# Retention stage: gate projections moved between scores, value products and sums; squares added on VectorE; the input norm's root carried by the rotary tables, decays and gates

## The reference

```python
h = rms_norm_2(x, mix_norm[i])                 # x * rsqrt(mean(x*x)) * gain
q, k, v, g = split(h @ w_in)                   # 4 heads: q, k 256 wide, v, g 512 wide
q = rotary(q, pos); k = rotary(k, pos) / 16
scores = (q . k) * decay                       # chunk-causal, decay by head
o = scores @ v
o = rms_norm_2(o, out_gain) * silu(g)          # norm over the 512 columns of a head
x = x + o @ w_o
```

## Time and profile before

| | |
|---|---|
| median of 3 runs | 3081.96 us (3081.77 to 3082.68) |
| profiled execution | 3082.99 us |
| its span, first to last instruction | 3081.2 us |
| mean granted TensorE clock | 0.982 |
| TensorE busy | 2969.8 us, 96% |
| VectorE busy | 1184.6 us, 38% |
| ScalarE busy | 569.9 us, 18% |
| GpSimd busy | 1822.2 us, 59% |

### The profile page before, as it was taken

One profiled execution on the slowest core, in us unless ns is written; L12 is line 12 of the kernel. 1 busy time (PEld: TensorE's weight loads), 2 busy tenths in 40 slices (PEclk: granted clock), 3 DMA queues, 4 the chain that ended last, 5 costly groups with the idle time before them and its releaser, 6 DMA issues.

```text
span 3081.2 us, 36748 instructions
## 1 busy us (share of the span) xinstructions
PE 2969.8 (96%) x13812; PEld 2373.5 (77%) x13812; DVE 1184.6 (38%) x1400; ACT 569.9 (18%) x787; POOL 1822.2 (59%) x1822
## 2 busy tenths in 40 slices
PE   6999998999998999999999989999999999999999
PEld 4677776888875677888878868878888777788887
DVE  3467224332435564432431321254233355543141
ACT  2442212100012443100011101120001344310000
POOL 4346444777782234777775645657777634477775
PEclk8899999999998999999999999999999999999999
DMA  3112211223231011223232212212222211122322
GB/s 116 55 55 69 82 62 48 96 84 111 86 105 35 26 41 41 96 84 103 94 122 82 73 64 82 82 69 91 93 98 91 76 60 54 55 96 87 102 96 84
DMA packets 37230, 242.16 MB, mean 79 GB/s; under 512 B 4128, under 2 KB 4256, under 8 KB 15136
## 3 DMA queue, kind: packets, MB, share of 16 engines
q1 hardware_dynamic: 36288, 237.19, 22.7%
q10 hardware_dynamic: 864, 3.89, 0.4%
HBM read 238.97 MB, written 2.10 MB: 78 GB/s over the span
## 4 chain that ended last, share of the span: by engine, by line
PE 90%; DVE 4%; ACT 2%; POOL 1%; issue 1%; DMA 1%; DVEq 1%; ACTq 0%; POOLq 0%; SPq 0%
PE ps L394 62%; PE ps L416 12%; PE ps L1291 1%; PE ps L1260 1%; PE ps L1086 1%; PE ps L1223 1%; PE ps L1103 1%; PE ps L1113 1%; POOL w_lo L659 1%; PE ps L676 1%; PE ps L1277 1%; PE ps L1304 1%; PE ps L753 1%; PE ps L1209 1%; PE ps L1074 0%
## 5 line engine op out<-in xcount | busy, mean ns | idle before, releaser
L655 POOL CAST w_hi<-raw 128x512 fp32r<-128x512 f32 (+1 forms) x909 | 580.1, 679 | 1221.5 <-PE ps L394 849.8
L659 POOL TENSOR_TENSOR w_lo<-raw,w_hi 128x512 fp32r<-128x512 f32 (+1 forms) x909 | 1242.2, 1396 | 20.2
L394 PE MATMUL ps<-h_hi,w_hi 128*128 128x512 f32 x1904 | 756.3, 397 | 18.2 <-DVE h_lo L1745 9.7
L394 PE MATMUL ps<-h_lo,w_hi 128*128 128x512 f32 x1904 | 745.5, 392 | 0.0
L394 PE MATMUL ps<-h_hi,w_lo 128*128 128x512 f32 x1904 | 745.0, 391 | 0.0
L394 PEld LDWEIGHTS ps<-h_hi,w_hi 128*128 128x128 f32 x1904 | 360.8, 189 | 99.1 <-DVE h_lo L1745 10.5
L394 PEld LDWEIGHTS ps<-h_lo,w_hi 128*128 128x128 f32 x1904 | 360.7, 189 | 76.6 <-issue 3.4
L394 PEld LDWEIGHTS ps<-h_hi,w_lo 128*128 128x128 f32 x1904 | 360.2, 189 | 76.1
L394 PE MATMUL ps<-a_hi,w_hi 128*128 128x512 f32 x816 | 320.8, 393 | 6.2 <-DVE x L1937 2.9
L394 PE MATMUL ps<-a_lo,w_hi 128*128 128x512 f32 x816 | 319.4, 391 | 0.0
L394 PE MATMUL ps<-a_hi,w_lo 128*128 128x512 f32 x816 | 319.4, 391 | 0.0
(11 more groups left out here) (274 smaller groups left out, 3632.8 us busy)
## 6 DMA issues: line engine op xcount, KB each, us to landing
raw<-weights SPq DMA_DIRECT2D x169, 1024.0 KB, 4.9
raw<-weights SPq DMA_DIRECT2D x64, 704.0 KB, 4.1
raw<-weights SPq DMA_DIRECT2D x8, 640.0 KB, 3.9
raw<-weights SPq DMA_DIRECT2D x8, 512.0 KB, 3.6
x<-x_in SPq DMA_DIRECT2D x1, 2048.0 KB, 8.9
x_out<-x SPq DMA_DIRECT2D x1, 2048.0 KB, 6.3
scr<-phase_ret ACTq DMA_DIRECT2D x1, 1536.0 KB, 9.0
scr<-phase_ssd ACTq DMA_DIRECT2D x1, 640.0 KB, 4.2
```

Of the source, the lines that this page charges most:

```text
L394: mm = pe.matmul(out_ap, a, b, start=(i == 0 and not begun), stop=(i == n - 1 and ended))
L655: ins = pool.tensor_copy(w_hi[:, slot, piece], raw[:, slot, piece])
L659: ins = pool.tensor_tensor(w_lo[:, slot, piece], raw[:, slot, piece], w_hi[:, slot, piece].bitcast(F32), ALU.subtract)
```

## The change

It does five things, all within the retention stage.

1. `ret` joins `late_rstd`. TensorE takes the squares' sum after the first q projection. The root goes into the tables: VectorE multiplies `cos` and `sin` by it once; the root by token, turned onto partitions by four one-column matmuls (`r_tok`), multiplies the decays; each gate bank is multiplied by it before Silu (`g_scaled`).
2. The gate projections are cut into four banks of 24 matmuls and moved: one between scores and value products, one behind the value products, then the sum of squares, then two.
3. Scores use banks 0 to 3, and so do the four value products, which stay in PSUM until VectorE has normed them. ScalarE's copy goes.
4. The four squares are added on VectorE; TensorE sums once instead of four times.
5. The waits for `x` being updated are moved behind the k projection. The loops over two heads are written out. ScalarE loads its function tables ahead by hand.

```diff
@@ late_rstd @@
-            return name.startswith("ffn") or name in ("sb", "mla")
+            return name.startswith("ffn") or name in ("sb", "mla", "ret")
@@ TensorE, ret @@
-                pe.wait_ge(s_res, 8 * (res_before["ret"] + half) + 2)
+                    def proj_g(r, half):
+                        if half == 0:
+                            chunk_split(c + 4 + r)
+                        mm = features(pe, ps[:, 4 + 2 * r + half, :], slot[4 + r], 256, half * P, P)
+                        mm.then_inc(s_used if half else s_rgp, 1)
...
-                    pe.wait_ge(s_rg, 2 * hd + 1)
+                    if hd:
+                        pe.wait_ge(s_roo, 4 * hd)
                     features2(pe, (0, 1), slot[0], h_ready("ret")).then_inc(s_used, 1)
+                    if hd == 0:
+                        norm("ret")
                     chunk_split(c + 1)
...
+                    if j == 0:
+                        pe.wait_ge(s_res, 8 * (res_before["ret"] + half) + 2)
+                    if hd == 0:
+                        pe.wait_ge(s_rstd, norm_of["ret"] + 1)
+                        for tb in range(TB):
+                            mm = pe.matmul(ps[:, 7, tb:tb + 1], norm_rstd[:, tb * P:(tb + 1) * P], ident[:, 0:1],
+                                           start=True, stop=True)
+                        mm.then_inc(s_rtok, 1)
+                    else:
+                        pe.wait_ge(s_rgs, 4 * hd)
+                        pe.wait_ge(s_rr, hd)
...
-                    for r in range(2):
-                        chunk_split(c + 4 + r)
-                        pe.wait_ge(s_rq, 2 * hd + r + 1)
-                        features(pe, ps[:, 2 * r, :], slot[4 + r], 256, 0, P)
-                        features(pe, ps[:, 2 * r + 1, :], slot[4 + r], 256, P, P).then_inc(s_used, 1)
...
+                    pe.wait_ge(s_rv, 2 * hd + 1)
+                    proj_g(0, 0)
+                    pe.wait_ge(s_rv, 2 * hd + 2)
+                    pe.wait_ge(s_rp, 4 * hd + 4)
                     for v in range(4):
...
-                        if v:
-                            mean(v - 1)
-                    mean(3)
+                    proj_g(0, 1)
+                    pe.wait_ge(s_rgs, 4 * hd + 1)
+                    pe.wait_ge(s_radd, hd + 1)
+                    pe.matmul(ps[:, 4, :], ones, r_sq[:, 0, :], start=True, stop=True).then_inc(s_rsum, 1)
+                    proj_g(1, 0)
+                    proj_g(1, 1)
...
+                pe.wait_ge(s_rr, 2 * half + 2)
+                pe.wait_ge(s_rgs, 8 * half + 6)
@@ ScalarE, ret @@
+                    act.preload_act_table_set(LN_EXP)
                     for v in range(4):
                         act.wait_ge(s_ro, 4 * hd + v + 1)
-                        act.wait_ge(s_rsum, 4 * hd + v + 1)
-                        act.activation(r_sq, ps[:, 6 + v % 2, :], ACT.Square)
-                        act.activation(r_oo[v], ps[:, 6 + v % 2, :], ACT.Copy).then_inc(s_rsq, 1)
+                        act.activation(r_sq[:, v, :], ps[:, v, :], ACT.Square).then_inc(s_rsq, 1)
+                    act.wait_ge(s_rsum, hd + 1)
+                    rstd(r_rstd, ps[:, 4, :], 1.0 / T).then_inc(s_rr, 1)
+                    act.preload_act_table_set("silu_and_others")
+                    for v in range(4):
+                        act.wait_ge(s_rgs, 4 * hd + v + 1)
+                        act.activation(r_g[:, v, :], r_g[:, v, :], ACT.Silu).then_inc(s_rg, 1)
@@ VectorE, ret @@
+                    def g_scaled(v):
+                        if v % 2:
+                            wait_used(c + 4 + v // 2)
+                        else:
+                            dve.wait_ge(s_rgp, 2 * hd + v // 2 + 1)
+                        dve.tensor_tensor(r_g[:, v, :], ps[:, 4 + v, :], norm_rstd, ALU.mult).then_inc(s_rgs, 1)
+
+                    def out_tile(v):
+                        dve.drain()
+                        dve.wait_ge(s_rg, 4 * hd + v + 1)
+                        dve.tensor_tensor(r_oo[v], r_oo[v], r_g[:, v, :], ALU.mult)
+                        split(a_hi[:, 4 * j + v, :], a_lo[:, 4 * j + v, :], r_oo[v]).then_inc(s_mix, 1)
+
+                    if hd == 0:
+                        dve.wait_ge(s_phase, 16 * (phase_order.index("ret") + 1))
+                        dve.wait_ge(s_rstd, norm_of["ret"] + 1)
+                        dve.tensor_tensor(cos, cos, norm_rstd, ALU.mult)
+                        dve.tensor_tensor(sin, sin, norm_rstd, ALU.mult)
+                    rotary(0, r_q)
+                    if hd == 0:
+                        dve.wait_ge(s_rtok, 1)
+                        dve.tensor_copy(r_tok, ps[:, 7, 0:TB])
+                    rotary(1, r_k)
...
+                    g_scaled(0)
+                    for v in range(1, 4):
+                        dve.wait_ge(s_rsq, 4 * hd + v + 1)
+                        ins = settled().tensor_tensor(r_sq[:, 0, :], r_sq[:, 0, :], r_sq[:, v, :], ALU.add)
+                    ins.then_inc(s_radd, 1)
+                    g_scaled(1)
+                    dve.wait_ge(s_rr, hd + 1)
                     for v in range(4):
...
+                        dve.scalar_tensor_tensor(r_oo[v], ps[:, v, :], param("ret_norm", 4 * hd + v), r_rstd,
+                                                 ALU.mult, ALU.mult).then_inc(s_roo, 1)
+                    g_scaled(2)
+                    for v in range(3):
+                        out_tile(v)
+                    g_scaled(3)
+                    out_tile(3)
```

More of the change, by code:

```diff
@@ L572, in build_program @@
         s_mT, s_mp, s_mo, s_mod = (sem("mla_scores_turned"), sem("mla_exp"), sem("mla_o"), sem("mla_o_scaled"))
-        used[0] = 0
+        used[0] = T
         r_rstd = take(T)
-        r_sq = take(T)
         r_t = take(2 * T, k=2)
+        r_tok = take(TB)
         assert used[0] <= base_norm
@@ L587, in build_program @@
         r_p = take(sum(RW))
-        s_rq = sem("ret_rotated")
-        s_rv, s_rg = sem("ret_v_copied"), sem("ret_g_silu")
+        r_sq = take(4 * T, v=4)
+        s_rtok, s_rq = sem("ret_rstd_turned"), sem("ret_rotated")
+        s_rv, s_rgp, s_rgs, s_rg = (sem("ret_v_copied"), sem("ret_g_product"), sem("ret_g_scaled"), sem("ret_g_silu"))
         s_rs, s_rp = sem("ret_scores"), sem("ret_scores_decayed")
-        s_ro, s_rsq, s_rsum, s_rr, s_rdone = (sem("ret_o"), sem("ret_square"), sem("ret_square_summed"),
-                                            sem("ret_rstd"), sem("ret_head_done"))
+        s_ro, s_rsq, s_radd, s_rsum, s_rr, s_roo = (sem("ret_o"), sem("ret_square"), sem("ret_squares_added"),
+                                                   sem("ret_mean"), sem("ret_rstd"), sem("ret_o_normed"))
         r_oo = [r_q[:, 0, :], r_q[:, 1, :], r_k[:, 0, :], r_k[:, 1, :]]
@@ L1178, in head @@
                     slot = [(c0 + r) % 2 for r in range(6)]
+                    def proj_g(r, half):
[3 more added lines that the diff above has]
+                        mm.then_inc(s_used if half else s_rgp, 1)
                     chunk_split(c)
-                    pe.wait_ge(s_rg, 2 * hd + 1)
+                    if hd:
+                        pe.wait_ge(s_roo, 4 * hd)
                     features2(pe, (0, 1), slot[0], h_ready("ret")).then_inc(s_used, 1)
+                    if hd == 0:
+                        norm("ret")
                     chunk_split(c + 1)
[L1184 to L1190, removed]
+                    for k in range(2):
+                        mm = features(pe, ps[:, 2 + k, :], slot[1], 256, k * P, P)
+                    mm.then_inc(s_used, 1)
+                    if j == 0:
[9 more added lines that the diff above has]
+                        pe.wait_ge(s_rr, hd)
                     for r in range(2):
                         chunk_split(c + 2 + r)
+                        if hd == 0 and r == 1:
+                            pe.wait_ge(s_rq, 2)
                         for tb in range(TB):
@@ L1226, in head @@
                         mm.then_inc(s_ro, 1)
-                        if v:
-                            mean(v - 1)
-                    mean(3)
-                with pe.Fori(0, 2) as j:
+                    proj_g(0, 1)
[4 more added lines that the diff above has]
+                    proj_g(1, 1)
+                for j in range(2):
                     head(j)
+                pe.wait_ge(s_rr, 2 * half + 2)
+                pe.wait_ge(s_rgs, 8 * half + 6)
             def stick(c0):
@@ L2134, in head, with rotary @@
                     c = c0 + 6 * j
-                    for r, dst in enumerate((r_q, r_k)):
+                    def rotary(r, dst):
                         dve.drain()
@@ L2145, in head @@
+                    rotary(1, r_k)
                     for kb in range(TB):
                         dve.wait_ge(s_rs, 4 * hd + kb + 1)
[L2147 to L2150, removed]
-                    for v in range(4):
[L2152 to L2157, removed]
@@ L2158, in head @@
-                    dve.drain().then_inc(s_rdone, 1)
```

(8 more changed lines are left out.)

20 lines of the change are left out of this document (3 added, 17 removed).

## The result

The changed kernel takes 3043.05 us, median of 4 runs (3042.76 to 3044.09), against 3082.05 us (3081.77 to 3082.68) beside it: ratio 0.9874, 95% interval [0.9857, 0.9891], 39.0 us faster. The forecast was 3047, its range 3041 to 3058. The profiled execution took 3044.09 us with a span of 3042.3 us, 38.9 less than the span before.

A forecast was written before the change was run, and what follows sets the result against it. TensorE, busy 96% of the span, was taken as the bound. The terms -16.8 - 6.3 + 0.8 - 1.9 - 10.7 = -34.9 us took the profiled 3082.99 us to 3048.1, median 3047, range 3041 to 3058.

The forecast's parts named there:

- Term 1: Each head's end: fewer sums and covered waits gain 4.2 us a head, -16.8 us over four heads.
- Term 4: First chunk of each residual: only tile 7 still late, by 1.1 us, 1.3 with restart; gain 10.7 us.
- Term 2: Stage's start: sum, wait and q projection fall from 20.7 to 14.4 us, -6.3; one-column matmuls add 0.8.
- The stretch of the earlier trace less the gate banks: Head's end, first score to what follows: 18.25 us before; scores, value products and one sum, 14.1 us after.
- The covers that I costed at nothing: Gate banks in each head, 5.44 us each, hide VectorE's decays (0.5 us left) and squares with additions (at most 3).
- The analogy with mla: Stage's start: it would begin as mla does behind a like ffn, 14.4 us for wait, q projection and sum.
- Term 3: Between the halves: moving the wait for `x` behind k's projection gains 1.9 us.
- The slack towards `s_roo`: Ahead of the next q projection: normed outputs end at M+4.3, gate banks at M+10.9; 6.6 us slack, no cost.
- A: Residuals: output tiles and GpSimd collide on every instruction, tile 7 comes 8.3 us late; 3061 us, chance 0.09.
- B: Stage's start gains nothing: TensorE idles for `h` or the split and its clock falls; 3053 us, chance 0.09.
- C: Whole stage: GpSimd becomes the bound, its split slowing past 10.9 us a chunk; slower than before, chance 0.03.
- D: Each head: a moved wait closes a ring of delays, additions come later than the gate bank covers; 3064 us, chance 0.04.

The follow-up runs named there:

- four_sums: Changed kernel with TensorE again summing the four squares itself in four matmuls, VectorE adding none: 3052.21 us, stage 435.1 us (+10.3).
- gates_before_sum: Changed kernel with the last two gate banks moved from behind the sum of squares to before it: 3067.76 us, stage 450.5 us (+25.7).
- copied_out: Changed kernel with ScalarE's copy of each value product put back, VectorE norming from that SBUF copy instead of PSUM: 3044.88 us, stage 427.3 us (+2.6).
- early_norm: Changed kernel with the norm before the first projection again, tables, decays and gates without the root: 3046.84 us, stage 429.8 us (+5.1).
- sum_uncovered: Changed kernel with the second gate bank moved before the value products, so the sum follows the last one directly: 3048.25 us, stage 431.8 us (+7.1).
- wait_x_first: Changed kernel with the wait for the updated x put back ahead of each half's first q projection: 3045.04 us, stage 426.4 us (+1.7).

## Why the prediction was right

The direction, the size and the places were right; the sum was 4 us short of the gain (-34.9 against -38.9 in the span). Terms 1 and 4 were too small by 1.8 and 2.9 us, term 2 was too large by 0.7. By the two traces the four terms are 18.6, 4.8, 1.9 and 13.6 us, together 38.9, so nothing is left for the parts that were not tested alone, such as the loops written out.

**Term 1, the heads.** Predicted -16.8. The second head of a half, from its first q matmul to the residual's first, went from 85.15 us to 80.5, 4 x 4.65 = -18.6. The three sums were sized well (2.6, measured by four_sums 2.58). The stretch of the earlier trace rows less the gate banks came to 13.9 us for 14.1, but in part by luck: scores, value products and sum took 4.24, 8.55 and 0.45 us, 0.8 less than the 4.4, 8.8 and 0.86 that I added up, and 0.7 that I had not counted came on top. That is the slow start of a projection behind a float32 matmul. Its first matmul is recorded with 0.79 us instead of 0.39, and two banks behind the sum take 11.33 us (1958.69 to 1970.02) where 10.88 would do. Before, this fell on q's projection. There it cost 0.3 us a head outside my stretch (11.21 us for q's two banks behind the sum), which I did not count as lost. Now it falls on the gates, and each gate bank between float32 products has 0.13 more. The covers that I costed at nothing are worth 0.76 us a head (decays), 1.8 (squares and additions) and, behind the sum, by far the most.

**Term 2, the start.** Predicted -6.3 + 0.8 = -5.5; -4.8 in the two traces (before, 8.35 us to the first matmul and a first head 1.3 us longer than the second; after, 1.2 and 3.6), 5.1 when undone alone. The analogy with mla held to 0.1 us: 1599.69 to 1614.07 is 14.4 us. The one-column matmuls took 0.80 (1625.40 to 1626.20). Of the missing 0.7 us, 0.45 are the slow restart behind the sum (11.33 for 10.88) and 0.1 that behind the one-column matmuls; before the change q's projection in the later heads had such a restart too, so the first head stood out by 1.3 us and not by the 1.5 of the clock.

**Term 3, between the halves.** Predicted -1.9; 1.7 when undone alone, 1.9 by the traces.

**Term 4, the residuals.** Predicted -10.7. To tile 7 the residuals took 16.06 and 16.24 us, now 9.52 each: -13.3, the whole of the wait, and to the residuals' end, with the restart behind tile 7, -13.6. This is the term that was mis-sized most. M is the start of the matmul behind the head's sum, 1754.19 in the second head. I had tile 7 ready at M+21.5 and wanted at M+20.4. It was ready at M+19.8 (1773.98 less 1754.19) and wanted at M+20.85. Tiles 4 to 6 were faster than I gave them, since GpSimd's next chunk starts only at M+11.7 and slows its neighbours mostly in its subtractions: 2.0 to 2.5 us for the first three tiles, 4.8 for the last. And the two gate banks took 11.3 us, not 10.9.

The slack towards `s_roo` (6.6 us predicted) was there: the normed outputs were complete at M+4.7 where I had M+4.3, 6.7 us ahead of the end of the two gate banks, and only gates_before_sum, which takes the cover away, brings that wait.

**The rivals.** A did not come: only tile 7 takes the slow time on all three instructions. Its ground is true, though, as copied_out shows where it strikes more instructions. The strictest reading, that such instructions take turns as wholes, is not shown: in copied_out four on VectorE and four on GpSimd lie within 7.0 us (1755.28 to 1762.31), where four of 0.75 and 5.0 us one after the other would be 8.0. B fell (early_norm). C: GpSimd's slowest chunk in the stage takes 9.3 us (1765.85 to 1775.14), under 10.9. D fell; `s_radd` is waited for only in sum_uncovered. The chances that I gave to the faster cases add up to 0.95, not 0.94.

## What to carry to other kernels

When one engine is the bound, look at each place where it waits for a short chain on the others and ask which of its own independent work can be put exactly there: here the same four gate banks, placed one, one and two, cover three chains, and with the last two placed before the sum 25.7 us of the 39 are lost again. Count a wait with what follows it: the waits of 4.2 and 5.6 us had a low clock behind them that cost 1.5 to 2.6 us more, those of 1.0 to 1.8 us had none. Where VectorE's other input is in SBUF and GpSimd is at work, an operand that can be read from PSUM should not be copied to SBUF first, even if the copy itself is hidden: here it cost 2.6 us.

## What the runs showed of the hardware

- Four multiplications on VectorE with one input in PSUM and one in SBUF took 2.73 us beside GpSimd; with both in SBUF, 5.87 us, and GpSimd's subtractions went from 5.0 to 6.7 us. The Trainium skill, SBUF — State Buffer, section "Who interferes with whom", says that a VectorE instruction with two SBUF inputs contends with a GpSimd instruction that reads SBUF, and one with at most one such input does not; both traces agree.
- By the same section of the Trainium skill a cast from SBUF to SBUF can contend too. It took 0.43 us with GpSimd idle and 1.36 beside it.
- TensorE's granted clock was 0.67 and 0.66 over the 4 us behind 4.2 and 5.6 us of idle time, so part of them at 1.2 instead of 2.4 GHz; behind the 1.0 us at the stage's start of the changed kernel it was 1.00, and so behind the 1.4 of wait_x_first, the 1.6 of sum_uncovered and the 1.8 of the earlier trace rows.
- The first matmul of rounded operands after a float32 matmul costs up to 0.45 us extra: 11.33 against 10.88 us for two banks.
- Four one-column float32 matmuls of 128 columns of weights are recorded with 0.95 us (0.80 to the start of the next matmul), more than four transposes of 128 columns, 0.63.
